# Output projection by token halves, with the norm and the first blocks of network two behind it; one SBUF plan for the last three phases; the load joined to network one

## The reference

```
h = concat(meta, x)                                       # 1040 x 1024
h = h + 0.5 * ffn1(rms_norm(h))                           # silu(u @ Wg) * (u @ Wup) @ Wdown, 2816 wide
h = h + token_mixing(rms_norm(h))                         # two attentions, gates, then @ w_out
h = h + 0.5 * ffn2(rms_norm(h))
return h[16:]
```

## Time and profile before

| | us |
|---|---|
| runs: median (lowest to highest of 3) | 2648.75 (2641.16 to 2656.07) |
| the profiled execution: time, span | 2638.91, 2636.9 |
| PE busy / DVE / ACT / POOL | 2439.4 (93%) / 1428.5 (54%) / 938.0 (36%) / 546.8 (21%) |
| mean granted TensorE clock | 0.955 of full |

### The profile page before, as it was taken

One profiled execution on the slowest core, in us unless ns is written; L12 is line 12 of the kernel. 1 busy time (PEld: TensorE's weight loads), 2 busy tenths in 40 slices (PEclk: granted clock), 3 DMA queues, 4 the chain that ended last, 5 costly groups with the idle time before them and its releaser, 6 DMA issues. The chain is left out here.

```text
span 2636.9 us, 37128 instructions
## 1 busy us (share of the span) xinstructions
PE 2439.4 (93%) x14204; PEld 2154.5 (82%) x14204; DVE 1428.5 (54%) x2001; ACT 938.0 (36%) x1557; POOL 546.8 (21%) x647
## 2 busy tenths in 40 slices
PE   5999999999969998978998979998979999999999
PEld 5999999999958887866787768887757787787887
DVE  6767655655457556533767652112147666656553
ACT  4332333333245444432444441112124333333432
POOL 0133300000033233321434453221200333000000
PEclk7999999999979999887989989999989999999999
DMA  4365532665230000010000011110322665326653
GB/s 172 123 206 195 187 136 91 236 221 180 83 128 1 25 25 1 1 33 10 4 7 4 4 41 49 50 51 1 129 104 80 210 215 194 132 100 244 227 189 115
DMA packets 123765, 277.00 MB, mean 105 GB/s; under 512 B 9361, under 2 KB 56337, under 8 KB 120289
## 3 DMA queue, kind: packets, MB, share of 16 engines
q1 hardware_dynamic: 123616, 274.97, 30.0%
HBM read 194.47 MB, written 80.33 MB: 104 GB/s over the span
## 5 line engine op out<-in xcount | busy, mean ns | idle before, releaser
L924 DVE TENSOR_TENSOR f_w_lo<-f_rw,f_w_hi 128x1024 fp32r<-128x1024 f32 x154 | 195.6, 1270 | 280.7 <-ACT f_w_hi L599 280.7
L762 PE MATMUL f_ps<-u_hi,f_w_hi 128*128 128x260 f32 (+1 forms) x1056 | 284.8, 324 | 32.2 <-DVE u_lo L861 15.5
L762 PE MATMUL f_ps<-u_lo,f_w_hi 128*128 128x260 f32 (+1 forms) x1056 | 282.5, 322 | 0.0
L762 PE MATMUL f_ps<-u_hi,f_w_lo 128*128 128x260 f32 (+1 forms) x1056 | 282.4, 322 | 0.0
L762 PEld LDWEIGHTS f_ps<-u_hi,f_w_hi 128*128 128x128 f32 x1056 | 178.1, 192 | 52.6 <-issue 32.6
L762 PE MATMUL f_ps<-f_far_hi,f_w_hi 128*128 128x260 f32 (+1 forms) x792 | 210.6, 320 | 7.9 <-DVE f_w_lo L924 7.9
L762 PE MATMUL f_ps<-f_far_lo,f_w_hi 128*128 128x260 f32 (+1 forms) x792 | 210.3, 320 | 0.0
L762 PE MATMUL f_ps<-f_far_hi,f_w_lo 128*128 128x260 f32 (+1 forms) x792 | 209.9, 319 | 0.0
L599 ACT CAST f_w_hi<-f_rw 128x1024 fp32r<-128x1024 f32 x154 | 160.7, 1046 | 107.5 <-PE f_ps L762 67.9
L762 PEld LDWEIGHTS f_ps<-u_lo,f_w_hi 128*128 128x128 f32 x1056 | 177.5, 191 | 14.3
L762 PEld LDWEIGHTS f_ps<-u_hi,f_w_lo 128*128 128x128 f32 x1056 | 177.6, 191 | 13.8
(11 more groups left out here) (378 smaller groups left out, 6127.0 us busy)
## 6 DMA issues: line engine op xcount, KB each, us to landing
f_rw<-in_gu SPq DMA_DIRECT2D x88, 512.0 KB, 4.7
f_rw<-kept_dsum SPq DMA_DIRECT2D x32, 704.0 KB, 5.5
f_rw<-kept_hid SPq DMA_DIRECT2D x33, 520.0 KB, 5.5
f_rw<-in_down SPq DMA_DIRECT2D x24, 704.0 KB, 4.1
f_rw<-kept_hid SPq DMA_DIRECT2D x33, 512.0 KB, 5.5
gt_raw<-in_gate SPq DMA_DIRECT2D x24, 512.0 KB, 3.5
h_in<-in_wd SPq DMA_DIRECT2D x11, 1024.0 KB, 5.8
kept_dsum<-h_in SPq DMA_DIRECT2D x44, 256.0 KB, 4.6
```

The costliest lines, as they stand in the source:

```text
L762: last = nc.tensor.matmul(out[:, b, 0:N], w[:, c], u[:, b * N:(b + 1) * N], start=(j in (0, 1, 5) and k == 0 and i == 0), stop=(k == 3 and ...
L924: nc.vector.tensor_tensor(slot(w_lo, st), src, slot(w_hi, st).bitcast(F32), ALU.subtract).then_inc(wlo_done, 1)
```

## The change

It touches three places.

1. **Head.** The load phase is gone. Network one's block loads the eight token tiles itself, into eight buffers that lie where u will be. It norms and scales the first 520 tokens first, the rest behind step 0. Scaled blocks go to buffers of their own (`U11`, `U21`) or, for the second half, over h. ACT does four of the eighteen copies of turned rows.
2. **Pairs.** The seven products of a pair get another order (`RAW_OF`, `PLACE`, the order of blocks in `gu`), with tiles `ps[(2, 0, 2, 0, 2, 0, 0)[j] + x]`. Steps 5 and 6, and step 1 of the next pair, now follow each other in `ps[0..1]`. The splits for `down` and the loads of raw weights move with it.
3. **Tail.** Gates, output projection and network two are one block with one SBUF plan. The projection runs over 16 units, eight output tiles for tokens 0 to 511, then eight for 512 to 1023, and loads each weight block twice. Its first three blocks are loaded and split inside the gate phase. Squares are summed by half; sum, root, spread, scaling and the splits of steps 0 and 1 of the first half stand between units 8 and 15, and the second half's sum and spread between the halves of steps 0 and 1.

The diff, cut to its core:

```diff
-RAW_OF = {0: 0, 5: 3, 6: 2}
+RAW_OF = {0: 0, 1: 1, 6: 3}
...
+PLACE = ((False, 2), (False, 1), (True, 0), (True, 1), (True, 2), (True, 3), (False, 0))
...
+        def s_buf(near, far, w, n):
+            if n == 0:
+                return far[:, 12 * W - SN:12 * W]
...
+            def start_from_rows():
+                sp.dma_start(g.ident[:, :], g.dram["ident"]).then_inc(start.ident_in, 16)
+                sp.dma_start(start.metain[:, :], g.dram["meta"]).then_inc(start.meta_in, 16)
+                for t in range(4):
+                    load_rows(t)
+                sp.dma_start(g.gains[:, :], g.dram["gains"]).then_inc(start.gains_in, 16)
+                load(0)
+                for t in range(4, QT):
+                    load_rows(t)
+                for m in range(1, 4):
+                    load(m)
+                sp.wait_ge(start.copied, 10)
+                save(0, slice(0, KD), 0)
+                load(4)
+                sp.wait_ge(start.copied_late, 4)
+                sp.wait_ge(start.copied, 14)
+                save(1, slice(0, 4), 1)
+                save(2, slice(4, KD), 1)
+                sp.dma_start(g.ones[:, :], g.dram["ones"]).then_inc(start.ones_in, 16)
+                sp.wait_ge(start.ones_in, 16)
...
+            def load_out(i):
+                if i >= 6:
+                    sp.wait_ge(start.wlo, i - 5)
+                sp.dma_start(start.raw(i), g.dram["wout"][i % KD]).then_inc(start.raw_in[i % 3], 16)
+
+            def start_from_product():
+                sp.wait_ge(start.gates_ready, 8 * KD)
+                load_h(0, 0)
+                load_out(3)
+                load_h(0, 2)
+                load_out(4)
+                load_h(0, 4)
+                load_out(5)
+                load_h(0, 6)
+                for m in range(0, KD, 2):
+                    load_h(1, m)
+                for i in range(6, 2 * KD):
+                    load_out(i)
+                    if i == 11:
+                        sp.wait_ge(start.added, KD)
+                        save(0, slice(0, KD), 0)
+                        sp.wait_ge(start.mixed_shut, 4 * KD)
+                        load(0)
+                        load(1)
+                    if i == 13:
+                        load(2)
+                        load(3)
+                load(4)
+                sp.wait_ge(start.added, KD + 4)
+                save(1, slice(0, 4), 1)
+                sp.wait_ge(start.added, 2 * KD)
+                save(2, slice(4, KD), 1)
+
...
 
...
+            if first:
+                start_from_rows()
+            else:
+                start_from_product()
...
+                    sp.wait_ge(add_done, 4 * p + 3)
+                    load(4 * p + 5)
                     sp.wait_ge(add_done, 4 * p + 4)
-                    load(4 * p + 5)
                     load(4 * p + 6)
+                    load(4 * p + 7)
...
                 if p + 2 < FP:
-                    sp.wait_ge(wlo_done, 7 * p + 6)
+                    sp.wait_ge(wlo_done, 7 * p + 7)
...
-                if p + 1 < FP:
-                    sp.wait_ge(wlo_done, 7 * p + 7)
-                    load(4 * p + 7)
...
+            sp.wait_ge(add_done, 4 * FP)
+            sp.wait_ge(wlo_done, STEPS - 5)
+            load_s(0)
             sp.wait_ge(b_stored[0], 48 * 5)
             sp.wait_ge(b_stored[1], 48 * 5)
-            sp.wait_ge(wlo_done, STEPS - 2)
+            sp.wait_ge(wlo_done, STEPS - 1)
...
+            if not first:
+                for i in range(3, 2 * KD):
+                    pool.wait_ge(start.whi, i - 2)
+                    nc.gpsimd.tensor_tensor(start.w_slot(w_lo, i), start.raw(i), start.w_slot(w_hi, i).bitcast(F32),
+                                            ALU.subtract).then_inc(start.wlo, 1)
...
-                if j in (0, 3, 5):
-                    act.wait_ge(u_done, {0: 0, 3: 8, 5: 12}[j] + 2 * q + 2)
+                if j in (0, 1, 4):
+                    act.wait_ge(u_done, {0: 0, 1: 4, 4: 12}[j] + 2 * q + 2)
...
+            if first:
+                act.preload_act_table_set("sqrt_and_others")
+                for t in range(4):
+                    rows_squared(t)
...
+                roots(0)
...
+                weight_hi(0)
+                spread_copy(0)
+                rows_squared(4)
+                rows_squared(5)
+                both(0)
+                rows_kept(10)
+                rows_kept(11)
+                rows_squared(6)
+                rows_kept(12)
+                rows_squared(7)
+                rows_kept(13)
+                roots(1)
+                both(1)
+                weight_hi(1)
+            else:
+                for i in range(2 * KD):
+                    out_hi(i + 2)
+                    if i:
+                        square_of(i - 1)
+                    if i == 9:
+                        roots(0)
+                    elif i == 10:
+                        spread_copy(0)
+                    elif i == 11:
+                        both(0)
+                    elif i == 13:
+                        both(1)
+                    elif i == 14:
+                        weight_hi(0)
+                weight_hi(1)
+                square_of(2 * KD - 1)
+                roots(1)
+            spread_copy(1)
+            snap(0, 0)
             weight_hi(2)
...
             snap(0, 1)
+            both(2)
             weight_hi(3)
-            u_hi(4, 0)
-            u_hi(4, 1)
-            snap(1, 0)
-            snap(1, 1)
-            u_hi(5, 0)
-            u_hi(5, 1)
+            both(3)
+            silu(1, 0)
+            silu(1, 1)
+            both(4)
             weight_hi(4)
-            u_hi(6, 0)
-            u_hi(6, 1)
             snap(2, 0)
+            both(5)
+            both(6)
...
             def product(st, x):
                 p, j = st // 7, st % 7
-                out = ps[(0, 2, 0, 2, 0, 2, 0)[j] + x]
+                out = ps[(2, 0, 2, 0, 2, 0, 0)[j] + x]
                 if x == 0:
                     pe.wait_ge(wlo_done, st + 1)
                 if j == 0 and p:
+                    pe.wait_ge(gate_done, 4 * p - 1 + x)
+                elif j == 1 and p:
                     pe.wait_ge(hid_done, 4 * p - 1 + x)
-                elif j == 1 and p:
-                    pe.wait_ge(gate_done, 4 * p - 1 + x)
+                elif j == 1 and first:
+                    pe.wait_ge(bc_copied, 1 + x)
                 elif j == 1:
-                    pe.wait_ge(bc_copied, 2)
-                elif j in (2, 3, 4):
-                    pe.wait_ge(snapped, 6 * p + {2: 1, 3: 3, 4: 5}[j] + x)
+                    pe.wait_ge(start.added, 2 * KD - 3 + 2 * x)
+                elif j == 2:
+                    pe.wait_ge(snapped, 6 * p + 1 + x)
+                elif j == 3:
+                    pe.wait_ge(gate_done, 4 * p + 1 + x)
+                elif j == 4:
+                    pe.wait_ge(snapped, 6 * p + 3 + x)
                 elif j == 5:
-                    pe.wait_ge(gate_done, 4 * p + 1 + x)
+                    pe.wait_ge(snapped, 6 * p + 5 + x)
...
+                pe.wait_ge(start.ident_in, 16)
+                for t in range(4):
+                    rows_turned(t)
+                pe.wait_ge(start.meta_in, 16)
+                for n in (8, 9):
+                    turn_rows(n, start.metain[:, :], META, 0)
+                rows_turned(4)
+                rows_turned(5)
+                spread_roots(0)
+                rows_turned(6)
+                rows_turned(7)
+                product(0, 0)
+                product(0, 1)
+                pe.wait_ge(start.copied_late, 4)
+                pe.wait_ge(start.copied, 14)
+                spread_roots(1)
+                product(1, 0)
+                product(1, 1)
+            else:
+                for i in range(2 * KD):
+                    out_unit(i)
+                    if i == KD:
+                        pe.wait_ge(start.sq_summed, KD - 1)
+                        sum_squares(0)
+                    elif i == KD + 1:
+                        spread_roots(0)
+                product(0, 0)
+                pe.wait_ge(start.sq_summed, 2 * KD - 2)
+                pe.wait_ge(bc_copied, 1)
+                sum_squares(1)
+                product(0, 1)
+                spread_roots(1)
+                product(1, 0)
+                product(1, 1)
+            for st in range(2, STEPS):
...
+                elif j == 3:
+                    raw_landed(dve, 4 * p + 1)
                     dve.wait_ge(add_done, 4 * p + 1)
                     if p:
                         dve.wait_ge(wlo_done, st - 4)
                     nc.vector.tensor_tensor(out, other, A11, ALU.subtract).then_inc(add_done, 1)
...
             def evacuate(st, x):
                 p, j = st // 7, st % 7
-                if st < 0 or j < 3:
+                if st < 0 or j not in (1, 4, 5, 6):
                     return
                 dve.wait_ge(prod_done, 2 * st + x + 1)
-                if j == 3:
+                if j == 1:
```

(39 more changed lines are left out.)

611 lines of the change are left out of this document (311 added, 300 removed).

## The result

| | before | after |
|---|---|---|
| median of 4 runs each (lowest to highest), us | 2646.36 (2641.16 to 2656.07) | 2601.52 (2599.84 to 2613.51) |
| the profiled execution: time, span, us | 2638.91, 2636.9 | 2599.84, 2597.7 |
| mean granted TensorE clock | 0.955 | 0.962 |

What follows compares the result with a forecast made beforehand. PE, busy 93%, was taken as the bound, losing time to idling or its lower clock. Tail 33.7 + pairs 11.3 + `down` 1.5 + head 7.9 = 54.4 us less: median 2648.75 to 2594 us, range 2579 to 2618.

Steps and rivals of the forecast that it cites:

- tail, gates to step 6: Output projection and network two's first seven steps: 181.5 us before, 148 expected, 33.7 us less (22 to 36).
- projection end / step 2 / step 3: In the tail: projection ends at 1928.5 us; step 2 starts 16.3 and step 3 26.4 us after that.
- head, end of step 6: Network one's start: step 6 ends at 88.9 us instead of 96.8, 7.9 us less (gain 4 to 10.4).
- waits for the multiply in the pairs: PE's nine waits ahead of step 0 for the multiply L946 that empties its tile, 11.3 us, would vanish.
- The split for `down` comes a step earlier, to a place of its own: up to 1.5 us less: In the pairs: moving this split earlier would save up to 1.5 us of the 1.48 us wait in front of `down`.
- new margin: In the pairs, `evacuate(5,0)` done 4.2 us after the step's start where step 6 wants it at 5.48: 1.3 us spare.
- the 11.3 us: Claimed gain in the pairs: the new tile order gives step 0 enough cover that L946 no longer stops PE.
- Two steps of cover: In the pairs: step 0's tile was last emptied in step 4, so L946 no longer stops PE; 11.3 us less.
- Rival 1: Pairs give little: POOL's down-weight sums block DVE, making `evacuate(5,0)` late; 11 us lost, 2605 us; chance 0.12.
- A wait of 5.9: Network two's start: PE would wait about 5.9 us ahead of step 5 for DVE's `weight_lo`.
- The small matmuls: In the tail: half of L803 and L813 stand in the projection, taken as 1.7 us at full clock, 3.5 if unchanged.
- four rivals: Pairs give little (0.12); DVE paces both starts, 2616 us (0.10); slower, 2677 us (0.03); no change (0.04).

Runs made afterwards that it cites:

- last_pair_late: Changed kernel with silu and evacuations of steps 4 and 5 ahead of the `down` splits in each network's last pair; median 2591.75 us, ratio to before 0.9798.
- old_cover: Changed kernel, but step 0 of each pair again waits for the multiply of step 6, as before the change; one run, 2618.40 us.
- no_pool_sums: Kernel before the change with POOL's four sums per block of down weights cut to 8 columns; one run, 2644.97 us.
- after_no_pool_sums: Changed kernel with POOL's four sums per block of down weights cut to 8 columns; one run, 2599.84 us.
- less_mixing: Changed kernel with ACT's copies for steps 2 and 3 and step 5's weight split earlier, plus two DVE weight sums per first pair cut to 8 columns; 2606.39 us.
- sum_later_head: Changed kernel with the first half's sum of squares one projection unit later and network one's second spread between step 0's halves; one run, 2603.51 us.
- all_four: Changed kernel with late last-pair `down` splits, early step 5 weight split and step 2 copy, later first-half sum, earlier second spread; median 2580.29 us, ratio to before 0.9756.
- low5_early: Changed kernel with ACT's second step 2 copy ahead of the casts and step 5's weight split one place earlier; median 2600.59 us, ratio to before 0.9853.
- norm_behind: Changed kernel with the first token half's norm factor, scaling and splits moved behind all 16 projection units; one run, 2623.12 us.

## Why the prediction was right, and where it was not

The time, 2601.5 against 2594, is inside the range. The forecast's mechanism held for the tail and the head. In the pairs the waits went, but mostly for another reason, and the last pair got slower. By its steps, in us:

| term | predicted | measured |
|---|---|---|
| tail, gates to step 6 | 148 | 151.5 |
| of it: projection end / step 2 / step 3 | 90.1 / +16.3 / +26.4 | 92.1 / +16.6 / +26.7 |
| head, end of step 6 | 88.9 | 91.1 |
| waits for the multiply in the pairs | 0 (before 11.3) | 0 |
| last pairs (last_pair_late) | 0 | +5.5 and +7.1 |
| `down` | -1.5 | 0 |

**How close it was.** The profiled execution was forecast at 2584.5 us and took 2599.8. The span fell by 39.2 of the 54.4 us. The 15.2 that are missing are, to within 0.2, 12.6 in the last pairs, 3.7 in the tail, 2.2 in the head and 1.3 at `down`, less 3.9 gained inside the pairs beyond the listed waits and 0.6 in the second stretch. The medians differ by 45 us only because the executions that were not profiled lie further above the profiled one before than after (median 7.5 us, against 1.7), so that the median came within 7.5 us of its forecast is in part luck.

**Right.** The projection starts with no stop and never waits for weights; the wait behind unit 8 (1.38, predicted 1.5); the waits of 3.85 and 2.86 ahead of steps 2 and 3; no wait for L946 and none at step 6 inside the pairs; 5.44 us a step there (5.48 predicted).

**Failed: "The split for `down` comes a step earlier, to a place of its own: up to 1.5 us less".** Nothing was asked about what stands behind it on DVE. The split waits for a load, the load stands on SP behind a store that waits for DVE's sums, and `evacuate(5, 0)`, whose new margin was only 1.3 us, is queued behind. The cost is 3.95 and 4.79 us of waits and 1.4 and 2.3 of lower clock behind them, shown by last_pair_late (5.5 and 7.1 us). The prediction had worked out that margin and named all queues of the pairs, but took the last pair as one of them.

**Right in size, wrong in its reason: the 11.3 us.** "Two steps of cover" explains 2.2 of them (old_cover). The waits came from POOL's blocking of DVE's sums (no_pool_sums), and in the new order the sums and POOL no longer meet. Rival 1 had looked at this blocking only as a loss to come; it was the cause of the waits before.

**Wrong place, right chain: the wait in the start.** A wait of 5.9 was foreseen at step 5, and 6.3 came in the middle of step 4, for `snap(2, 1)` on ACT. From the end of the projection to the end of step 6 it took 59.4 us, 57.7 predicted: off by 1.7 only, because the chain of DVE and ACT ends where it did. Moving the copies shows it: 0.4 to 2.3 us came back in each network, not 6.

**Mis-sized.** The small matmuls and the clock behind the stop: a wait of 1.38 us was counted, the 1.6 us of lower clock behind it was not (tail, 92.1 against 90.1). The last `down` stretch lost 1.7: the 1.48 of the earlier trace rows went and 1.49 came back at the third unit, whose weights SP loads behind stores again.

None of the four rivals occurred. The pairs hold 3.9 us more gain than the listed waits, 2.6 of it in network two. It is not clock: behind the waits for L946 the matmuls stood 0.23 us apart, as at full clock. There the change of pairs itself was slower before: the steps on its two sides took some 5.60 and 5.55 us without their waits, every other step 5.44. In the changed kernel all take 5.44. old_cover has the longer two only where its three waits are.

## What to carry to other kernels

When a piece of work that waits for a load is moved up in one engine's program, list what now stands behind it and who has the smallest margin there, and do it again for the last turn of the loop, where the order differs. Before crediting a gain to a new buffer assignment, look at whether the late instruction was itself slow in the trace: here the same instruction had two durations, and what ran beside it was the cause. Where a wait moves on by one place each time it is removed, the chain behind it is the bound: here a new order gave back 2.3 us at most of a wait of 6, and taking 2.1 us of work off DVE another 1.4.

## What the runs showed of the hardware

**A short stop can cost clock, but its length does not tell.** Behind unit 8 TensorE idled 1.38 us, ran ten matmuls at full clock, eight of them small, and then some eight at the lower level, 0.43 us apart in place of 0.23:

```profile
1887.24 0.63 PE L73 MATMUL f_ps<-u_hi,f_w_hi 128*128 128x512 f32 x1
1887.67 0.63 PE L74 MATMUL f_ps<-u_hi,f_w_lo 128*128 128x512 f32 x1
```

The same stop with the same instructions stands in eight profiled executions, of the changed kernel and seven edits of it. In six the lower level followed; in after_no_pool_sums and less_mixing it did not, and the projection was 1.6 us shorter. In sum_later_head and all_four, without the stop, the clock stayed at 1.00. Behind the wait of 2.86 us at 1952.70 came five matmuls at the full clock, then some eight at the lower. But in the kernel before the waits for L946 in network two, 1.1 to 2.1 us long, had no lower clock behind them:

```profile
2219.24 0.40 PE L762 MATMUL f_ps<-u_hi,f_w_lo 128*128 128x512 f32 x1
2219.48 0.40 PE L762 MATMUL f_ps<-u_lo,f_w_hi 128*128 128x512 f32 x1
```

These two stand 0.3 and 0.54 us behind the end of a wait of 2.13 us.

**Identical code varied by 22 us with the granted clock.** The attentions between 1140 and 1570 us, in low5_early, then in norm_behind:

```profile
1140.00:1570.00 430.00, 377.66 (x2064) 307.94 (x2065) 258.53 (x548) 179.55 (x438) 166.01 (x314) 0.92 0.05 15
```

```profile
1140.00:1570.00 430.00, 385.32 (x2021) 313.55 (x2022) 249.62 (x544) 170.25 (x425) 152.08 (x307) 0.87 0.03 9
```

At a clock of 0.92 PE did 2064 matmuls in the window, at 0.87 it did 2021, and the second stretch took 1327.7 and 1349.9 us. No edit touches it, so a single execution says little about an edit of 5 us unless it is read by stretches. What made the granted clock differ is not shown.
